# Attention scores in the head order 0 4 1 5 2 6 3 7, and small transposes issued as transposes, in a two-layer encoder kernel

## The reference, cut to what matters

```python
for l in range(DEPTH):                       # DEPTH = 2, SEQ = 1024, D_MODEL = 1024
    z = _rmsnorm(x, norm1_g[l]) @ w_in[l]
    mq, mk, mv, mi, mf, mo, aq, ak, av = jnp.split(z, split_idx, axis=-1)
    ...
    hm = _mlstm_chunkwise(mq, mk, mv, i_pre, f_pre)     # b = cumsum(log_sigmoid(f)); running maxima
    ha = _swa_sinks(aq, ak, av, sinks[l])
    x = x + jnp.concatenate([hm, ha], axis=-1) @ w_out[l]
    x = x + jnp.square(jax.nn.relu(_rmsnorm(x, norm2_g[l]) @ w_ff1[l])) @ w_ff2[l]

# in _swa_sinks, G = 4 query heads to each of the 2 key heads:
s = jnp.einsum('bcqhgd,bckhd->bhgcqk', qb, k_band) * (A_HEAD_DIM ** -0.5)
```

## Time and profile before

| | us |
|---|---|
| median of three runs | 2165.57 |
| lowest and highest run | 2163.51, 2165.97 |
| span of the profiled execution | 2163.3 |
| PE busy in it | 2106.8 (97%) |
| DVE, ACT, POOL busy | 1397.2, 856.4, 964.2 |
| stage A, second and third column group, layer 0 | about 69.9 to 141.3 |
| stage B, layer 0 | about 141.3 to 310 |
| stage B, layer 1 | about 1212.1 to 1380 |

### The profile page before, as it was taken

One profiled execution on the slowest core, in us unless ns is written; L12 is line 12 of the kernel. 1 busy time (PEld: TensorE's weight loads), 2 busy tenths in 40 slices (PEclk: granted clock), 3 DMA queues, 4 the chain that ended last, 5 costly groups with the idle time before them and its releaser, 6 DMA issues.

```text
span 2163.3 us, 32423 instructions
## 1 busy us (share of the span) xinstructions
PE 2106.8 (97%) x10964; PEld 1752.3 (81%) x10964; DVE 1397.2 (65%) x1676; ACT 856.4 (40%) x1435; POOL 964.2 (45%) x701
## 2 busy tenths in 40 slices
PE   7999999999999999999999999999999999999998
PEld 7888877888788878888888887788878888788886
DVE  5037876477777787676630488654767777867664
ACT  5134443255666632121241343432666666322120
POOL 4235514324555456464541455134155445556552
PEclk9999999999999999999999999999999999999999
DMA  5222235416667789767442223344257766996763
GB/s 211 88 102 71 79 115 186 167 44 218 238 232 250 262 338 352 291 250 293 175 135 88 91 79 116 132 152 146 98 184 254 257 236 234 381 349 258 279 246 146
DMA packets 222799, 423.11 MB, mean 196 GB/s; under 512 B 24296, under 2 KB 158184, under 8 KB 214512
## 3 DMA queue, kind: packets, MB, share of 16 engines
q1 hardware_dynamic: 153664, 346.82, 45.1%
q10 hardware_dynamic: 69040, 75.05, 9.9%
HBM read 268.60 MB, written 153.22 MB: 195 GB/s over the span
## 4 chain that ended last, share of the span: by engine, by line
PE 74%; DVE 11%; issue 7%; ACT 5%; POOL 1%; DMA 1%; ACTq 0%; DVEq 0%; SPq 0%; POOLq 0%
PE ps L1805 27%; PE ps L1527 10%; PE ps L1457 10%; PE ps L1756 9%; PE ps L1617 7%; PE ps L1437 4%; DVE uf L2212 3%; ACT w1s L1037 2%; ACT uf L1051 2%; PE ps L1428 1%; DVE wo L2085 1%; PE ps L1551 1%; DVE uf L2282 1%; DVE sS L2230 1%; ACT uf L1053 1%
## 5 line engine op out<-in xcount | busy, mean ns | idle before, releaser
L1805 PE MATMUL ps<-w2s,uk 128*128 128x512 f32 x2688 | 612.9, 390 | 5.4 <-DMA uk<-uD 2.9
L1805 PEld LDWEIGHTS ps<-w2s,uk 128*128 128x128 f32 x2688 | 503.2, 188 | 114.3 <-issue 4.5
L2322 DVE TENSOR_TENSOR xs<-ps,xs 128x1024 f32<-128x1024 f32 x208 | 253.9, 1221 | 180.8 <-PE ps L1805 178.4
L1756 PE MATMUL ps<-hT,w1s 128*128 128x512 f32 x1344 | 317.6, 392 | 5.9 <-DVE uf L2282 3.2
L1756 PEld LDWEIGHTS ps<-hT,w1s 128*128 128x128 f32 x1344 | 250.3, 188 | 68.0 <-DVE uf L2282 12.6
L1379 POOL TENSOR_TENSOR w2s<-raw,w2s 128x1024 fp32r<-128x1024 f32 x64 | 188.4, 2957 | 248.6 <-ACT w2s L1149 248.6
L1375 POOL TENSOR_TENSOR w1s<-rawf,w1s 128x512 fp32r<-128x512 f32 x112 | 151.3, 1360 | 216.2 <-ACT w1s L1037 216.2
L1527 PE MATMUL ps<-hT,whi 128*128 128x512 f32 x768 | 244.0, 399 | 0.0
L1756 PE MATMUL ps<-tT,w1s 128*128 128x512 f32 x1008 | 237.3, 389 | 0.0
L1756 PEld LDWEIGHTS ps<-tT,w1s 128*128 128x128 f32 x1008 | 189.1, 188 | 39.4
L1457 PE MATMUL ps<-ahi,hT 128*128 128x512 f32 (+1 forms) x768 | 213.0, 361 | 3.3 <-DVE hT L1853 3.3
(11 more groups left out here) (216 smaller groups left out, 3105.0 us busy)
## 6 DMA issues: line engine op xcount, KB each, us to landing
uk<-uD SPq DMA_DIRECT2D x64, 1024.0 KB, 7.8
raw<-in_wstream SPq DMA_DIRECT2D x100, 512.0 KB, 5.9
uk<-uD SPq DMA_DIRECT2D x64, 768.0 KB, 5.9
rawf<-in_wstream SPq DMA_DIRECT2D x64, 512.0 KB, 4.3
uD<-uh ACTq DMA_DIRECT2D x64, 512.0 KB, 6.3
uD<-uf SPq DMA_DIRECT2D x64, 512.0 KB, 7.6
uD<-uh ACTq DMA_DIRECT2D x64, 384.0 KB, 4.2
uD<-uf SPq DMA_DIRECT2D x64, 384.0 KB, 6.8
```

The lines of the kernel that those rows point to most:

```text
L1756: mm = pe.matmul(ps[:, bank, :], w, x[:, k, :], start=(first and k == 0 and i == 0), stop=(k == 3 and i == 2), skip_group_check=True)
L1805: mm = pe.matmul(ps[:, bank + tp, :], u, w2s[r][:, w, k, :], start=(r in (1, 2, 5) and k == 0 and i == 0), stop=(k == 1 and i == 2), skip_ ...
L2322: V.tensor_tensor(y, ps[:, bank:bank + 2, :], y, ALU.add).then_inc(y_acc, 1)
```

## The change

Two edits, both on PE's instruction stream. `rows_t` and `rows_m` issue the same 16 and 8 operations as transposes in place of matmuls with the identity. `scores` takes its heads in the order 0 4 1 5 2 6 3 7, so that two heads in succession use different partition halves and different PSUM banks. No wait and no semaphore changes, and no other engine's program.

```diff
                     for t in range(NT):
-                        pe.matmul(ps[0:MH, SB + t // 4, (t % 4) * P:(t % 4) * P + P], bN[:, t * MH:(t + 1) * MH], ident[:], start=True, stop=True)
-                        mm = pe.matmul(ps[0:MH, TB + t // 4, (t % 4) * P:(t % 4) * P + P], aN[:, t * MH:(t + 1) * MH], ident[:], start=True, stop=True)
+                        pe.transpose(ps[0:MH, SB + t // 4, (t % 4) * P:(t % 4) * P + P], bN[:, t * MH:(t + 1) * MH], ident[:])
+                        mm = pe.transpose(ps[0:MH, TB + t // 4, (t % 4) * P:(t % 4) * P + P], aN[:, t * MH:(t + 1) * MH], ident[:])
                     mm.then_inc(a_row, 1)
                 def rows_m():
                     pe.wait_ge(a_neg, l + 1)
                     for t in range(NT):
-                        mm = pe.matmul(ps[:, OB + 1, 64 + t * MH:64 + (t + 1) * MH], Mneg[:, t * P:(t + 1) * P], ident[0:MH, 0:MH], start=True, stop=True)
+                        mm = pe.transpose(ps[:, OB + 1, 64 + t * MH:64 + (t + 1) * MH], Mneg[:, t * P:(t + 1) * P], ident[0:MH, 0:MH])
                     mm.then_inc(a_mn, 1)
...
-                        for h in range(AH):
+                        for h in (0, 4, 1, 5, 2, 6, 3, 7):
                             b0, m = DH * (h // 4), h % 4
```

## The result

The changed kernel takes 2153.07 us (median of five runs, 2150.49 to 2155.02) against 2165.57 us (five runs, 2161.99 to 2166.29): a ratio of 0.9941, with a 95% interval of 0.9931 to 0.9951, 12.5 us or 0.6% faster. The forecast was 2153.8, range 2149.8 to 2160.0. The profiled execution of the changed kernel took 2155.02 us with a span of 2152.8, the slowest of the five.

What follows compares the result with a forecast made beforehand. PE was taken to bound the kernel, busy 2106.8 of 2163.3 us, except where qk_t(1) waits for DVE. Gains of 3.5 + 1.9 + 1.6 + 4.8 = 11.8 us off the median 2165.57 gave 2153.8 us, range 2149.8 to 2160.0.

Steps and rivals of the forecast that it cites:

- rows_t: Stage A, 16 operations a layer: one pass of 0.109 us each as transposes, saving 1.75 us a layer, 3.5 us in both.
- rows_m: Stage A, between the projection's two sets of 96 matmuls: half of 16 records go, 0.94 us a layer, 1.9 in both.
- scores: Stage B: alternating heads let the upper half start early, 0.47 us a call, 4.8 us in all.
- the first rival: Stage A, small transposes with four loaded columns: run in two passes like matmuls, costing 3.5 us, time 2157.3; chance 0.13.
- The bound from the projection's pace: Stage A, eight remaining small operations at 0.057 us each: upper end of the gain, 1.4 us a layer, 2.8 in all.
- The clock: Layer 1, behind the small operations between the projection's matmuls: the fall to half clock doesn't come, 1.6 us gained.
- the third rival: Clock falls in more places, such as step 2's longer qk_t(1) wait or the shortened rows_t; 2161.9 us; chance 0.09.
- the prediction's last sign of being wrong: Anywhere in the changed profile: stretches at half clock appear where there are none now.
- the second: Stage B, new head order brings nothing, PE's limit on instructions in hand decides; costs 4.8 us, time 2158.6; chance 0.11.
- the fourth rival: Stage B, alternating heads don't overlap and PE empties at each change of half; slower, 2170.3 us; chance 0.04.
- the split of the calls: Stage B: scores(1)'s 8 calls give 3.8 us, scores(0) 0.9 in step 0, 0.1 in step 1, nothing in steps 2 and 3.
- The sum: Whole kernel: 3.5 + 1.9 + 1.6 + 4.8 = 11.8 us, taken off the median 2165.57, 0.54% faster.

## Why the prediction was right, step by step

**rows_t** was put at 1.75 us a layer and gave 1.92 (3.588 to 1.664 us). A transpose takes the 0.109 us that p_t had shown, one record each; the first rival, two passes, did not happen. The Trainium skill, TensorEngine Tiling (Array Packing), Restrictions, has column tiling switch off transpose mode for FP32; nothing of the kind shows for these transposes with output on 4 partitions, but the trace gives only their loaded block, 128*4, and not whether the array was split for them. The 0.17 us more are at the end: the projection now starts 0.03 us after the last transpose's start, where 0.2 us lay before.

**rows_m** was undersized: 0.94 us a layer was forecast and 1.29 measured (1.874 to 0.588 us). The term kept the old 0.117 us for each of the eight that stay; they take 0.073. The bound from the projection's pace, 0.057, was the nearer end.

**The clock** behind rows_m went as forecast: no fall behind the new rows_m in any of the twelve layers profiled with it, against four of eight with the old one. The new piece is both shorter and made of transposes, and no run tells which of the two does it. That the 1.6 us would then be in hand was wrong for the execution as a whole: falls came up elsewhere, as the third rival said, though not where it said, one behind step 3's wait and two in the MLP, none in step 2 and none behind rows_t. By the prediction's last sign of being wrong, half-clock stretches where there were none, this step failed. The falls are a matter of chance as well: in the ten profiles the clock fell behind eight of the sixteen waits of step 3 of 1.73 us and more, and behind the same wait of 2.50 us in one layer of the changed kernel and not in the other.

**scores**: 0.47 us a call was taken and 0.49 measured, so the second and the fourth rival are out, and the split of the calls held: scores(1) and step 0 pay, steps 1 to 3 don't. The waits there were forecast at some 0.4, 0.84 and 2.2 us and are 0.42, 0.74 and 2.50; the last is 0.3 us longer than the arithmetic, for a reason that stays open. It varies: it is 2.22 us with the head order alone.

**The sum** of 11.8 us stands beside 12.5 in the medians and 10.5 in the profiled spans; that it came so near is in part luck. In the two profiles the stages that were touched gave 14.1 us, 2.3 more than the sum: rows_t, rows_m and scores some 11.3 instead of 10.2 (3.85, 2.57 and 4.9, the 0.49 us of ten calls), less some 0.5 us of the longer waits, and most of the rest is the fall behind step 3 of layer 0, some 1.5 us, which was there before and is gone. What the sum didn't have is the 3.5 us lost in the stretches with the MLP, and they are the clock's. PE does wait longer for `uk`, 2.9 to 5.1 us, but it no longer waits for DVE's `xs` some 7 us later. The MLP's second product, before and after, with records, busy time and mean, and behind the second bar the idle time ahead of it:

```profile
L1805 PE MATMUL ps<-w2s,uk 128*128 128x512 f32 x2688 | 612.9, 390 | 5.4 <-DMA uk<-uD 2.9 <-DVE xs L2320 2.3 <-DVE xs L2322 0.2
```

```profile
L1806 PE MATMUL ps<-w2s,uk 128*128 128x512 f32 x2688 | 616.3, 391 | 5.2 <-DMA uk<-uD 5.1
```

PE is not idle longer, it is busy 3.4 us longer, with both half-clock stretches in it. The kernel with qk_t(1) moved and the old head order is the counterpart: it waits 4.7 us for `uk`, has no fall, and the two stretches take 841.71 + 771.52 = 1613.2 us, as before (840.82 + 772.37; 0.9 us more in layer 0, 0.9 less in layer 1). So the longer wait by itself shows no cost over the two layers; what goes with it is the chance of a fall. In the ten profiles the clock fell behind seven of the twelve single waits for `uk` of 1.97 us and more, and behind none of the eight of 1.68 us and less.

Why the wait grew is open. In the ten profiles its two times together are 2.9 to 3.8 us where the stretch from rows_t to stage B takes 49 us or more, the kernel with four times the transposes among them (3.1), and 4.2 to 5.1 us where it takes 46. In layer 0 the load is issued 6.7 us earlier, with PE, and its later half lands 15.4 us after its issue where it took 14.1. Why its landing should know of stage A's length no run here shows.

## What to carry to other kernels

Small matmuls on different partition halves run side by side only when the other half's work is near enough in the instruction stream; alternating halves cut these calls by a third without a single instruction less. Before counting such a gain, look at what stands behind each call: ten of sixteen paid here, and moving the waiting transposes a few matmuls back brought some 7 us more, by the ratios 0.9941 and 0.9908, of which 6.4 show in stage B. A transpose in place of a matmul with the identity halved the records here, and the time followed because PE was what bounded those places. A change of clock elsewhere can be as large as any of these gains: before and after differ by 3.4 us at half clock in two single profiles, so compare the touched stage with itself, and look at the granted clock in it, before judging by the whole time.

## What the runs showed that was not expected

PE started matmuls of the upper half ahead of earlier ones of the lower half, past six records that had not started, and no farther in the old order; with two heads ahead of it, head 4 starts 0.02 us after head 0. A transpose that moves four columns takes 0.073 us of rows_m where a pass of the matmul took 0.117 (0.588 us for 8, 1.874 for 16). The granted clock fell behind a stretch of 1.87 us of four-column matmuls in four of eight layers, at about 1.6 us a time, and behind none of the twelve stretches of 0.59 us of four-column transposes. And PE's wait for `uk`, which grew by 2.2 us, did not lengthen PE's idle time ahead of that product (5.4 us before, 5.2 after), because a later wait went.
